# The banded attention layer of a four-layer kernel: its first 22 units issued in pairs on TensorE, and the finished heads copied one unit later

## The chip, the cores and the metric

One core of a Trainium2 chip. The kernel is timed in microseconds (us) of device time for one execution of the whole program; less is better. The kernel before has a median of 2338.8 us over 3 runs (2338.51 to 2340.18).

## The reference, cut to what matters

The program computes four mixing layers over 512 tokens of width 1024 (a dilated one, a differential one, an mLSTM with RG-LRU, and a banded attention with sinks), the last two each followed by attention over a memory and an MLP. The change touches the banded layer alone. It has 16 query heads of 64 channels, 4 key heads, and a window of 128 tokens:

```
qkv = u @ w_qkv
q, k = rotary(q), rotary(k)
# block j of 128 queries sees the keys of blocks j-1 and j
s = jnp.einsum('blkgd,bckd->bkglc', qb, kb) * scale
s = jnp.where(band, s, -inf)
m = jnp.maximum(jnp.max(s, axis=-1), sink)
p = jnp.exp(s - m[..., None])
den = jnp.sum(p, axis=-1) + jnp.exp(sink - m)
ob = jnp.einsum('bkglc,bckd->blkgd', p, vb) / den
out = ob @ w_o
```

## The kernel before

The work is written out by hand for each engine; the engines meet only at counting semaphores, and each engine takes its instructions in the order in which they are written.

**Units.** The banded layer is cut into 32 units. Unit k has head pair t = k // 4 and query block n = k % 4, so two heads of 128 queries. Its scores are 256 keys wide, or 128 where n is 0. Four kinds of work of a unit run on TensorE (PE):

- S, the scores: `unit_scores`, line 671; two matmuls of 64 rows, one for each head.
- T, the transposes of the probabilities: `transposes`, line 678; four of 128x128 (two where n is 0) into bank `TB0 + n % 2`.
- V, the values: `values` by `chain`, line 683; matmuls of 64 columns, one half of the array for each head, into bank `OB`.
- Q, a quarter of a projection tile: `quarter`, called by `between`, line 614; six matmuls 128x512 of the split product (`uh`, `ul` by `wh`, `wl`). 24 quarters make the last six tiles of the q projection, and all go through the one bank `XB`. From unit 22 on, `between` issues pieces of the output projection instead (`begin`, line 614 too).

**The order on PE** (`attend`): for each n: S(n+2), Q(n+2) or pieces, T(n), V(n-1).

**VectorE (DVE)**, in its loop over k: the masked maximum mx(k+1) (L2174), then for unit k the wait for its exponentials, the sum and reciprocal (L2891, L2893), the scaling of the probabilities (L2896) and a drain (L2897) that releases T(k). I write R(k) for the start of L2891 of unit k. Behind it come, by k % 4, the turning of the next head pair (`sw_cos`, `sw_sin`, `sw_turned`: L2180, L2186, L2189) and `result(t)` (L2882), the copy of a finished head pair from bank `OB` into `F`. V of the first unit of head pair t waits for `result(t-1)` (`y_before`). From k = 21 on DVE also makes the low parts of finished heads (`split_lo`, L2131).

**ScalarE (ACT)**, in its loop over k: ex(k+1), the exponentials (L1975, L1977); where k % 4 is 1, `take` (L1542), the copy of the tile in `XB`; pt(k), the copy of the transposes from PSUM into `spt` (L1529); where k % 4 is 1, `split_g` (L1378), two halves of a weight tile; from k = 20 on the high parts of finished heads (L1989). `spt` has two buffers, for even and odd k, and pt waits for the values that last read its buffer:

```
def spt(k): return wk(13312 + 512 * (k % 2))

def pt(U, dst, src):
    act.wait_ge(pt_psum, U + 1)
    wait(act, pv_done, U - 1)
    nc.scalar.activation(dst, src, ACT.Copy).then_inc(pt_ready, 1)
```

`pv_done` counts the units whose V is finished, so pt(k) needs T(k) and V(k-2). ACT's order is `ex(k + 1)` and then `pt(k)`. On PE, T(k) waits for pt(k-2) and V(k) for pt(k). S of a unit k up to 24 waits for mx(k-2), of a later one for mx(k-1). The first quarter of a tile waits for the `take` of the tile before it.

**GpSimd (POOL)** makes the low half of each weight tile (L573); in this layer it starts when DVE has finished the fourth unit of a head pair.

Of the kernel before, what the change touches and what calls it, by code (L numbers as in the profile page):

```python
# [27 lines left out]
TT = S // P  # L28
# [56 lines left out]
def build(nc, x, mem, positions, tiles, cols, post, consts, masks, maskd_in, rgw, out, upto="all"):  # L85
    ctx = ExitStack()
    with ctx:
# [45 lines left out]
        PS = ctx.enter_context(nc.psum_tensor("PS", [P, 8, 512], F32))  # L133
# [226 lines left out]
        def sq_(t): return wk(3072 + 512 * t)  # L360
# [246 lines left out]
        def _(pe):  # L607
# [66 lines left out]
            def transposes(U, ps, srcs, ahead=1):  # L674
                wait(pe, pt_ready, U + 1 - ahead)
                pe.wait_ge(probs_ready, U + 1)
                for n, a in enumerate(srcs):
                    last = nc.tensor.transpose(ps[:, n * P:(n + 1) * P], a, ident)  # L678
                last.then_inc(pt_psum, 1)
# [337 lines left out]
                u_ev = out_projection("diff_out", 6)  # L1017


            def attend(name, units, between=None, tiles=None):  # L1020

                U = UNIT[name]

                def values(n):
                    pe.wait_ge(pt_ready, U + n + 1)
                    wait(pe, y_taken, units[n]["y_before"])
                    for out, pairs in units[n]["values"]:
                        last = chain(out, pairs)  # L1030
                    last.then_inc(pv_done, 1)

                def unit_scores(n):
                    if "tile" in units[n]:
                        pe.wait_ge(lin_evac, units[n]["tile"])
                    if "low" in units[n]:
                        pe.wait_ge(cross_lo, units[n]["low"])
                    if "turned" in units[n]:
                        pe.wait_ge(aux_taken, units[n]["turned"])
                    if units[n].get("keys") is not None:  # L1040
                        pe.wait_ge(units[n]["keys"], 32)
                    scores(U + n, units[n]["scores"], ahead=1 if n == 0 else units[n].get("ahead", 2))

                if between is not None:
                    between(-2)
                    between(-1)
                if tiles is not None:
                    tiles(0)
                unit_scores(0)
                if tiles is not None:  # L1050
                    tiles(1)
                unit_scores(1)
                if tiles is not None:
                    tiles(2)
                for n, un in enumerate(units):
                    if n + 2 < len(units):
                        unit_scores(n + 2)
                    if between is not None:
                        between(n)
                    transposes(U + n, PS[:, TB0 + n % 2, :], un["probs"], ahead=2)  # L1060
                    if n >= 1:
                        values(n - 1)
                if between is not None:
                    between(len(units))
                values(len(units) - 1)

            if on("ev"):
# [16 lines left out]
                U = UNIT["ev"]  # L1084
# [202 lines left out]
            if on("sw"):  # L1287
                b = BASE["sw"]
                first_tiles(b, u_sw, taken=y_evac, evacuated=FF_Y0[0] + 57)
                for m in (4, 5):  # L1290
                    feature_tile(b + m, slot_of(b + m), m % 2, LIN["sw"] + m)
                    a = m - 2
                    pe.wait_ge(lin_evac, LIN["sw"] + a + 1)
                    for t in range(TT):
                        last = nc.tensor.transpose(PS[:, SV0 + a, t * P:(t + 1) * P],
                                                   svt(a)[:, t * P:(t + 1) * P], ident)
                    last.then_inc(aux_ready, 1)

                def quarter(n):

                    m, q = 6 + n // 4, n % 4
                    slot = slot_of(b + m)
                    if q % 2 == 0:
                        pe.wait_ge(lo_ready, 2 * (b + m) + q // 2 + 1)
                    if q == 0 and m > 6:
                        pe.wait_ge(lin_evac, LIN["sw"] + m)
                    for k in (2 * q, 2 * q + 1):
                        ks = slice(k * P, (k + 1) * P)
                        last = three(PS[:, XB, :], w_of(wh, slot)[:, ks], w_of(wl, slot)[:, ks],
                                     uh[:, k, :], ul[:, k, :], k == 0, k == KT - 1)  # L1310
                        if m == 11 and k < KT - 1:
                            last.then_inc(rows_read, 1)
                    if q == 3:
                        last.then_inc(tile_used, 1)

                def sw_unit(t, n):
                    l, lo = t // 2, max(n - 1, 0) * P
                    w = (n + 1) * P - lo
                    nt = w // P
                    k = 4 * t + n  # L1320
                    return dict(
                        scores=[(PS[:, sw_bank(k) + m, 0:w], sq_(t)[64 * m:64 * m + 64, n * P:(n + 1) * P],
                                 sk(l, m)[:, lo:lo + w], True, True) for m in range(2)],
                        keys=keys_mirrored[l // 2] if t % 4 == 0 and n == 0 else None,
                        probs=[ssm(k)[:, m, e * P:(e + 1) * P] for m in range(2) for e in range(nt)],
                        y_before=Y0["sw"] + t,
                        ahead=1 if k > 24 else 2,
                        turned=AUX["sw"] + t + 5,
                        values=[(PS[64 * m:64 * m + 64, OB, n * P:(n + 1) * P],
                                 [(sv[:, lo // P + e, 64 * l:64 * l + 64],  # L1330
                                   spt(n)[:, (m * nt + e) * P:(m * nt + e + 1) * P]) for e in range(nt)])
                                for m in range(2)])

                u_out = 8 * (c.add("u") - 1)

                def between(n):
                    if n < 22:
                        quarter(n + 2)
                        if n == -1:
                            pe.wait_ge(lin_evac, LIN["sw"] + 6)  # L1340
                        return
                    if n == 22:
                        pe.wait_ge(lin_evac, LIN["sw"] + 12)
                    at = (0, 1, 3, 4, 6, 9, 11, 13, 15, 17, 18, 22)[n - 22:n - 20]
                    begin(BASE["sw_out"], u_out, SW_EARLY[at[0]:at[1]], MOVED_MEM)

                attend("sw", [sw_unit(t, n) for t in range(8) for n in range(TT)], between)
                begin(BASE["sw_out"], u_out, SW_EARLY[22:34], MOVED_MEM)
            if on("ff1"):
                mlp(1, cross(1, out_projection("sw_out", 2, True)))  # L1350
# [665 lines left out]
        def _(dve):  # L2016
# [171 lines left out]
            def sw_turned(dst):  # L2188
                v.tensor_tensor(dst, stmp, dst, ALU.subtract)  # L2189
                v.drain().then_inc(aux_taken, 1)  # L2190
# [670 lines left out]
            if on("sw"):  # L2861
# [18 lines left out]
                def result(t):  # L2880
                    dve.wait_ge(pv_done, UNIT["sw"] + 4 * t + 4)
                    v.tensor_copy(F[:, t, :], PS[:, OB, :]).then_inc(y_taken, 1)  # L2882
# [3 lines left out]
                for k in range(32):  # L2886
                    if k < 31:
                        mx(k + 1)
                    w = P if k % 4 == 0 else 2 * P
                    dve.wait_ge(exp_ready, UNIT["sw"] + k + 1)  # L2890
                    v.tensor_tensor(rdn(k), den(k), sinkx(k), ALU.add)  # L2891
                    step()
                    v.reciprocal(rdn(k), rdn(k))  # L2893
                    step()
                    for m in range(2):
                        v.tensor_scalar(ssm(k)[:, m, 0:w], ssm(k)[:, m, 0:w], rdn(k)[:, m:m + 1], None, ALU.mult)  # L2896
                    v.drain().then_inc(probs_ready, 1)  # L2897
                    t = k // 4 + 1
                    if k % 4 == 0 and t < 8:
                        sw_sin(sq_(t), 4 + t)  # L2900
                    if k % 4 == 1:
                        if t > 1:
                            result(t - 2)
                        if t < 8:
                            sw_turned(sq_(t))
                    if k % 4 == 3 and t < 7:
                        sw_cos(5 + t)
                    heads = {21: (0, 1), 22: (1, 2), 23: (2, 3), 26: (3, 4), 27: (4, 5), 28: (5, 6), 30: (6, 7)}.get(k)
                    if heads is not None:
                        split_lo(*heads)  # L2910
# [174 lines left out]
```

## Time and profile before

| | |
|---|---|
| median of 3 runs | 2338.8 us (2338.51 to 2340.18) |
| the profiled execution | 2339.67 us |
| its span, first to last instruction | 2337.9 us |
| PE busy | 2293.1 us, 98% |
| DVE, ACT, POOL busy | 63%, 52%, 51% |
| mean granted TensorE clock | 0.998 |
| first scores of the banded layer | 1687.71 us |
| T(3), T(21), T(31) start | 1700.74, 1756.41, 1790.54 us |

Times inside the span are counted from its start. A row of the timeline gives the start, the duration, the engine, the line, the operation, the tiles, and in brackets the idle time in front of it and what ended it. Matmuls overlap, so the distance of two starts, and not the duration, is the time that a matmul takes from the next. A bracket is missing where the engine was not idle.

### The profile page before, as it was taken

The page shows a single profiled execution, that of the slowest core. Times are in us where ns is not written, and L with a number is a line of the kernel's source. Part 1 is how long each engine was busy: PE and PEld are TensorE (multiplying, and loading weights), DVE is VectorE, ACT ScalarE, POOL GpSimd, SP SyncE. Part 2 cuts the span into 40 slices and gives each one's busy share as a digit, 9 for nine tenths or more (in the row PEclk, how much of TensorE's full clock was granted, in tenths as well). Part 3 has the DMA queues.
Part 4 walks back from the last instruction along what each step waited for, and adds up shares of the span by engine and source line. Part 5 has one row for each costly group of instructions (what it writes and reads, how often), then busy time and mean ns, then how long its engine had stood idle before and what let it go on. Part 6 is the DMA issues. An engine that isn't in the chain of part 4 may idle for free.

```text
span 2337.9 us, 39043 instructions
## 1 busy us (share of the span) xinstructions
PE 2293.1 (98%) x13234; PEld 1907.9 (82%) x13234; DVE 1463.5 (63%) x2476; ACT 1209.9 (52%) x2606; POOL 1197.8 (51%) x834
## 2 busy tenths in 40 slices
PE   8999999999999999999999999999999999999998
PEld 7888888888877778778898988888766998988886
DVE  5554555555667776773554666787685624667686
ACT  5343334334655556654644754544576744645453
POOL 4544344442443334433662478786422742587885
PEclk9999999999999999999999999999999999999999
DMA  5333333332432222222531224233323431233331
GB/s 191 118 102 101 96 104 109 100 100 64 140 95 91 90 67 83 85 71 77 166 122 64 91 82 133 83 113 95 91 69 104 143 101 55 91 121 96 99 109 72
DMA packets 126554, 232.82 MB, mean 100 GB/s; under 512 B 17200, under 2 KB 17456, under 8 KB 126384
## 3 DMA queue, kind: packets, MB, share of 16 engines
q1 hardware_dynamic: 123536, 220.08, 29.8%
q10 hardware_dynamic: 2848, 10.49, 1.3%
q8 instruction: 105, 1.72, 0.3%
q14 instruction: 65, 0.53, 0.1%
HBM read 208.48 MB, written 2.10 MB: 90 GB/s over the span
## 4 chain that ended last, share of the span: by engine, by line
PE 64%; issue 18%; POOL 9%; DVE 5%; ACT 2%; DVEq 1%; ACTq 1%; DMA 0%; POOLq 0%
PE PS L614 56%; POOL wl L573 8%; PE PS L683 3%; PE PS L671 2%; POOL w L573 2%; PE PS L678 1%; PE PS L638 1%; DVE H L2141 1%; DVEq L2022 1%; DVE work L2174 0%; DVEq L2175 0%; DVE ul L2131 0%; ACT work L1402 0%; DMA raw<-tiles_dram 0%; DVE work L2055 0%
## 5 line engine op out<-in xcount | busy, mean ns | idle before, releaser
L573 POOL TENSOR_TENSOR wl<-raw,wh 128x512 fp32r<-128x512 f32 x502 | 716.6, 1451 | 848.9 <-ACT wh L1378 457.5
L614 PE MATMUL PS<-uh,wh 128*128 128x512 f32 (+1 forms) x2088 | 761.1, 365 | 1.9 <-DVE ul L2074 0.9
L614 PE MATMUL PS<-uh,wl 128*128 128x512 f32 (+1 forms) x2088 | 747.6, 358 | 0.0
L614 PE MATMUL PS<-ul,wh 128*128 128x512 f32 (+1 forms) x2088 | 746.9, 358 | 0.0
L614 PEld LDWEIGHTS PS<-uh,wh 128*128 128x128 f32 x2088 | 396.3, 190 | 76.8 <-issue 14.8
L614 PEld LDWEIGHTS PS<-uh,wl 128*128 128x128 f32 x2088 | 396.1, 190 | 58.2
L614 PEld LDWEIGHTS PS<-ul,wh 128*128 128x128 f32 x2088 | 396.5, 190 | 54.0 <-issue 0.5
L573 POOL TENSOR_TENSOR wl<-diagonals,wh 128x512 fp32r<-128x512 f32 x212 | 295.4, 1417 | 177.2 <-ACT wh L1378 137.5
L614 PE MATMUL PS<-wh,forms 128*128 128x512 f32 x784 | 241.3, 389 | 0.0
L1378 ACT ACTIVATE wh<-raw 128x512 fp32r<-128x512 f32 x312 | 178.7, 622 | 95.8 <-PE PS L614 84.4
L1542 ACT ACTIVATE work<-PS 128x512 f32<-128x512 f32 x120 | 71.7, 598 | 297.7 <-PE PS L614 228.9
L614 PE MATMUL PS<-wh,uh 128*128 128x512 f32 x448 | 179.3, 400 | 2.8 <-DVE ul L2131 2.7
L614 PE MATMUL PS<-wl,uh 128*128 128x512 f32 x448 | 174.9, 390 | 0.0
L614 PE MATMUL PS<-wh,ul 128*128 128x512 f32 x448 | 174.6, 390 | 0.0
L1378 ACT ACTIVATE wh<-diagonals 128x512 fp32r<-128x512 f32 x212 | 122.1, 623 | 98.9 <-PE PS L614 94.1
L614 PEld LDWEIGHTS PS<-wh,forms 128*128 128x128 f32 x784 | 147.2, 188 | 30.6
L2795 DVE TENSOR_TENSOR work<-work,PS 128x1024 f32<-128x1024 f32 x84 | 102.5, 1220 | 103.2 <-PE PS L614 101.9
L614 PE MATMUL PS<-wl,forms 128*128 128x512 f32 x392 | 152.5, 389 | 0.0
L1523 ACT ACTIVATE work<-work,stat 128x512 f32<-128x512 f32 (+3 forms) x160 | 95.6, 599 | 75.9 <-DVEq L2175 73.9
L1363 ACT ACTIVATE wh<-raw 128x512 fp32r<-128x512 f32 x190 | 109.6, 624 | 14.0 <-issue 11.4
L614 PEld LDWEIGHTS PS<-wh,uh 128*128 128x128 f32 x448 | 84.1, 188 | 25.7 <-issue 9.3
L2209 DVE TENSOR_TENSOR work<-work,cst 128x512 f32<-128x512 f32 x64 | 95.8, 1496 | 10.4 <-DMA work<-work 9.4
(278 smaller groups left out, 3512.2 us busy)
## 6 DMA issues: line engine op xcount, KB each, us to landing
raw<-tiles_dram SPq DMA_DIRECT2D x534, 256.0 KB, 2.7
diagonals<-tiles_dram SPq DMA_DIRECT2D x212, 256.0 KB, 3.0
work<-work SPq DMA_DIRECT2D x296, 64.0 KB, 2.0
gB<-post_dram ACTq DMA_DIRECT2D x8, 512.0 KB, 3.9
H<-x_dram SPq DMA_DIRECT2D x4, 512.0 KB, 5.9
H<-x_dram ACTq DMA_DIRECT2D x4, 512.0 KB, 5.2
work<-mem_dram ACTq DMA_DIRECT2D x2, 1024.0 KB, 7.2
out_dram<-H ACTq DMA_DIRECT2D x4, 512.0 KB, 2.7
```

What stands on the lines that cost most here:

```text
L573: nc.gpsimd.tensor_tensor(w_of(wl, slot)[:, hc], src[:, hc], w_of(wh, slot)[:, hc].bitcast(F32), ALU.subtract).then_inc(lo_ready, 1)
L614: last = nc.tensor.matmul(out, a, b, start=start and m == 0, stop=stop and m == 2, skip_group_check=goes_on)
L638: last = nc.tensor.transpose(half_ps(half, k, banks)[:, t * P:(t + 1) * P], xn[:, 2 * half + t, k * P:(k + 1) * P], ident)
L671: ins = nc.tensor.matmul(o, q, k, start=first, stop=last)
L678: last = nc.tensor.transpose(ps[:, n * P:(n + 1) * P], a, ident)
L683: last = nc.tensor.matmul(out, a, b, start=n == 0, stop=n == len(pairs) - 1)
L1363: nc.scalar.activation(w_of(wh, slot)[:, hc], raw[:, raw_slot, hc], ACT.Copy).then_inc(hi_ready, 1)
L1378: nc.scalar.activation(w_of(wh, slot)[:, hc], src[:, hc], ACT.Copy).then_inc(hi_ready, 1)
L1523: last = nc.scalar.activation(sm, sm, ACT.Exp, bias=bias, scale=-1.0, accum_out=d)
L1542: nc.scalar.activation(dst, PS[:, bank, 0:width], ACT.Copy).then_inc(lin_evac, 1)
L2209: v.tensor_tensor(placed(dst), plain(swp(a)), plain(sinT), ALU.mult)
L2795: v.tensor_tensor(sums[i], sums[i], region, ALU.add).then_inc(y_evac, 1)
```

## The change

`attend` gets `pairs`, and the banded layer is called with 11. For n = 0, 2, ..., 20 PE now issues S(n+2), S(n+3), then Q and T(n), Q and T(n+1), and then V(n-2), V(n-1) (none in the first pair). Unit 22 has V(20) and V(21) behind its transposes, and from there the order is as before. On DVE, `result(t - 2)` moves from the iterations k % 4 = 1 to k % 4 = 2, behind the probabilities of that unit; `sw_turned` stays. ACT, POOL and the DMA queues have no edit, and no buffer is added.

```diff
-            def attend(name, units, between=None, tiles=None):
+            def attend(name, units, between=None, tiles=None, pairs=0):
...
-                for n, un in enumerate(units):
+                for n in range(0, 2 * pairs, 2):
+                    unit_scores(n + 2)
+                    unit_scores(n + 3)
+                    for k in (n, n + 1):
+                        between(k)
+                        transposes(U + k, PS[:, TB0 + k % 2, :], units[k]["probs"], ahead=2)
+                    if n:
+                        values(n - 2)
+                        values(n - 1)
+                for n in range(2 * pairs, len(units)):
                     if n + 2 < len(units):
                         unit_scores(n + 2)
                     if between is not None:
                         between(n)
-                    transposes(U + n, PS[:, TB0 + n % 2, :], un["probs"], ahead=2)
+                    transposes(U + n, PS[:, TB0 + n % 2, :], units[n]["probs"], ahead=2)
+                    if pairs and n == 2 * pairs:
+                        values(n - 2)
                     if n >= 1:
                         values(n - 1)
...
-                attend("sw", [sw_unit(t, n) for t in range(8) for n in range(TT)], between)
+                attend("sw", [sw_unit(t, n) for t in range(8) for n in range(TT)], between, pairs=11)
...
-                    if k % 4 == 1:
-                        if t > 1:
-                            result(t - 2)
-                        if t < 8:
-                            sw_turned(sq_(t))
+                    if k % 4 == 1 and t < 8:
+                        sw_turned(sq_(t))
+                    if k % 4 == 2 and t > 1:
+                        result(t - 2)
```

## Rows read from the trace of the kernel before

**Rows 1.** Busy time by window: four units in steady state, then units 22 to 25.

```profile
1716.25:1728.60 12.35, 12.35 (x84) 8.56 (x82) 10.21 (x37) 8.91 (x31) 3.01 (x2) 1.00 0.22 64
...
1757.64:1772.34 14.70, 11.12 (x76) 7.25 (x73) 12.50 (x43) 11.22 (x36) 3.44 (x2) 1.00 0.38 126
```

**Rows 2.** Timeline of PE in steady state.

```profile
1703.99 0.38 PE L678 MATMUL PS<-cst,work 128*128 128x128 f32 x2
...
1707.55 0.44 PE L683 MATMUL PS<-work 128*64 128x128 f32 x4
1707.92 0.49 PE L671 MATMUL PS<-work 64*128 64x128 f32 x4
1708.34 0.50 PE L614 MATMUL PS<-uh,wh 128*128 128x512 f32 x1
1708.68 0.40 PE L614 MATMUL PS<-ul,wh 128*128 128x512 f32 x1
...
1709.83 0.60 PE L678 MATMUL PS<-cst,work 128*128 128x128 f32 x4
1710.36 0.67 PE L683 MATMUL PS<-work 128*64 128x128 f32 x8
1710.96 0.70 PE L671 MATMUL PS<-work 64*128 64x256 f32 x4
```

**Rows 3.** Timeline of DVE: R(0), R(1), R(2), R(11) and R(23).

```profile
1690.31 0.16 DVE L2891 TENSOR_TENSOR stat<-stat 128x2 f32<-128x2 f32 x1 [0.24 <-ACTq L1979]
...
1693.01 0.16 DVE L2891 TENSOR_TENSOR stat<-stat 128x2 f32<-128x2 f32 x1
...
1696.18 0.16 DVE L2891 TENSOR_TENSOR stat<-stat 128x2 f32<-128x2 f32 x1
...
1723.15 0.16 DVE L2891 TENSOR_TENSOR stat<-stat 128x2 f32<-128x2 f32 x1 [0.32 <-ACTq L1979]
...
1761.23 0.16 DVE L2891 TENSOR_TENSOR stat<-stat 128x2 f32<-128x2 f32 x1 [0.37 <-ACTq L1979]
```

**Rows 4.** Timeline of ACT: pt(8); take, ex(11); ex(23), pt(22).

```profile
1716.75 0.38 ACT L1529 ACTIVATE work<-PS 128x256 f32<-128x256 f32 x1 [1.09 <-PE PS L678]
...
1719.63 0.60 ACT L1542 ACTIVATE work<-PS 128x512 f32<-128x512 f32 x1 [1.11 <-PE PS L614]
...
1721.64 0.51 ACT L1975 ACTIVATE work<-work,stat 128x256 f32<-128x256 f32 x1
...
1759.72 0.50 ACT L1975 ACTIVATE work<-work,stat 128x256 f32<-128x256 f32 x1
...
1761.33 0.60 ACT L1529 ACTIVATE work<-PS 128x512 f32<-128x512 f32 x1 [0.15 <-issue]
```

**Rows 5.** Timeline of PE: the starts of T(1), T(3) and T(21).

```profile
1694.30 0.63 PE L678 MATMUL PS<-cst,work 128*128 128x128 f32 x4 [0.22 <-DVEq L2897]
...
1700.74 0.60 PE L678 MATMUL PS<-cst,work 128*128 128x128 f32 x4
...
1756.41 0.60 PE L678 MATMUL PS<-cst,work 128*128 128x128 f32 x4
```

**Rows 6.** Timeline of PE, last units: V(24), S(28), V(28), V(31).

```profile
1771.23 0.44 PE L683 MATMUL PS<-work 128*64 128x128 f32 x4
1772.34 0.49 PE L671 MATMUL PS<-work 64*128 64x128 f32 x4 [0.67 <-DVEq L2175]
...
1785.02 0.44 PE L683 MATMUL PS<-work 128*64 128x128 f32 x4
...
1794.67 0.67 PE L683 MATMUL PS<-work 128*64 128x128 f32 x8
```

**Rows 7.** Timeline of DVE, last units: R(26), R(30) and result(7).

```profile
1772.29 0.16 DVE L2891 TENSOR_TENSOR stat<-stat 128x2 f32<-128x2 f32 x1
...
1784.91 0.16 DVE L2891 TENSOR_TENSOR stat<-stat 128x2 f32<-128x2 f32 x1
...
1795.40 0.69 DVE L2882 COPY F<-PS 128x512 f32<-128x512 f32 x1 [5.03 <-PE PS L683]
```

## The prediction

> **What bounds the kernel now.** I read the page first: PE is busy 98% of the span, so what counts is what lengthens PE's own stream or makes it stand. The stretch in question is 1688 to 1795 us. By windows, four units in steady state take 12.35 us and PE is busy for 12.35 of them [rows 1]; units 22 to 25 take 14.70 with 11.12 busy. The timeline of DVE shows that PE has a partner that is nearly as full: R(k) waits for ACT only once in four units, in a gap of 0.32 us [rows 3]. A gap between two such steps is 0.20 us where nothing is late, and every fourth mx is followed by one of 0.40, so a real wait of 0.2 us is all that DVE has left in 12.35 us. In units 22 to 27 DVE leads: S(28) stood 0.67 us for its drain [rows 6]. So the two questions are what the new order costs or saves on PE, and whether it makes DVE or ACT later. The third view is ACT's: pt always stood for PE's transposes (pt(8): 1.09 us, released by L678) and never for values [rows 4]. That is what the change alters.
>
> **PE's own stream.** No matmul is added or removed; only neighbours change. From [rows 2]: a full S lasts 0.70 and a half one 0.49, so two halves of columns differ by 0.21 and S itself is 0.42; the half S is followed after 0.42, where 0.21 would do, so a change of form costs 0.21 there. V: 0.67 less 0.44 is 0.23, the half V is followed after 0.37, so 0.14 is for the change. T: 0.60 less 0.38 is 0.22 for two transposes, so four are 0.44, and V comes after 0.53: 0.09. Q's first matmul is followed after 0.34, its duration is 0.50 against 0.40 of the next: 0.10. Sum 0.54 us for a unit. A pair meets S, T-to-V and V once instead of twice; between T and Q both fill the whole array. No row here stands for S behind S or V behind V; the bounds are nothing saved and 0.54 us a pair, and I take the upper one. Eleven pairs: 6 us less work for PE. PE then needs about 12.35 - 2 x 0.54 = 11.3 us for four units.
>
> The Trainium skill, TensorEngine Tiling (Array Packing), section Tiling Modes, says the same of the mechanism: a change of tiling mode, not of tile, drains TensorE. By it the change should be faster by what the switches cost; the trace agrees with the switches but not that PE alone sets the pace, and this is the first rival below.
>
> **DVE's own stream.** Same instructions, `result` one iteration later. Behind `result` the next mx comes after one TENSOR_TENSOR step with no drain in front, so some 0.1 us may go, and with the 0.2 of waiting DVE could run four units in about 12.05 us. So even without any new wait the gain is limited to 0.3 x 4.5 = 1.4 us, not 6.
>
> **The new wait.** pt(k) needs V(k-2) finished, since `spt` has two buffers. Before, V(k-2) stands ahead of T(k) on PE, so the wait is always over. Now, for even n, V(n-2) stands behind T(n+1). T(n+1) needs probabilities of unit n+1; and on ACT pt(n) stands ahead of ex(n+2). Queued behind the waiting pt(n) are, in order: ex(n+2), take, pt(n+1), split_g, ex(n+3); DVE waits for the two ex. So a serial chain closes once a pair: T(n+1) on PE, V(n-2) on PE, pt(n) and ex(n+2) on ACT, R(n+2) and the scaling on DVE, and so on to T(n+3). Nothing hides it, for DVE had 0.2 us left.
>
> Prices of its steps. T to V: 0.53, and 0.03 more if T had stood (0.63 long against 0.60 [rows 2, 5]): 0.56. V start to a reader of its result: 1795.40 - 1794.67 = 0.73 [rows 6, 7], a half V 0.23 less, 0.50. pt: a copy of 512 columns is 0.60 long and the next starts 0.11 before its end, 0.49; of 256 columns 0.38 long [rows 4], 0.28. ex to R: 1723.15 - 1721.64 = 1.51 [rows 3, 4]; with 128 columns two activations are 0.11 shorter, 1.29. ex to ACT's next: 1761.33 - 1759.72 = 1.61. take, pt and split_g to the next ex: 1721.64 - 1719.63 = 2.01. R to T on PE: 1694.30 - 1693.01 = 1.29 [rows 3, 5]. R(4j) to R(4j+1): 1693.01 - 1690.31 = 2.70 on DVE.
>
> From T(4j+3) to T(4j+5): 0.56 + 0.50 (V(4j) is a half one) + 0.49 + 1.29 gives R(4j+4) at 2.84; DVE then needs 2.70 (ACT would be ready at 1.55 + 1.39 + 0.49 + 1.51 = 4.94, earlier than 5.54), and 1.29: 6.83 us.
>
> From T(4j+1) to T(4j+3): 0.56 + 0.73 + 0.28 = 1.57 for the start of ex(4j+2); here ACT is the slow one: + 1.61 + 2.01 + 1.51 + 1.29 = 7.99 us. DVE (R(4j+2) at 3.08 and then about 2.6 to R(4j+3) with `result`) would be ready at 5.7, ACT at 6.70.
>
> PE has time for its pair in both: V V, S S, Q, T, Q add up to 1.0 + 1.1 + 1.5 + 0.5 + 1.4 = 5.5 us behind T; only the quarter that waits for `take` (done 3.7 us after T(4j+1)) comes near, and then T(4j+3) could start at 7.1, before 7.99. POOL starts when the fourth unit is ready, and its 3.0 us now lie beside DVE's idle time; I cost that at nothing, up to 0.6 us in four units in favour.
>
> Four units: 6.83 + 7.99 = 14.8 us instead of 12.35. The first pair has no V and no wait: R(2) stays at 1696.18 [rows 3], S(5) needs mx(3) just before it, and 0.63 + 1.49 + 0.45 + 1.38 puts T(3) at 1700.1, against 1700.74 [rows 5]: 0.6 us ahead. From T(3) to T(21) there are five intervals of 6.83 and four of 7.99, 66.1 us, where the trace has 1756.41 - 1700.74 = 55.67. T(21) is late by 66.1 - 55.7 - 0.6 = 9.8 us.
>
> The pair of unit 20 closes the chain once more, with one high part behind pt(20) and two behind split_g (copies of 512 columns, 0.5 each by the row of take): R(23) comes at 1.57 + 0.5 + 1.61 + 2.01 + 1.0 + 1.51 = 8.2 us after T(21); before 1761.23 - 1756.41 = 4.8. So 3.4 more, 13.2 in all.
>
> **The moved copy.** While V(n-2) stands behind T(n+1), the copy one iteration later is early enough. From unit 22 on the old order holds, and V(24) stands on PE right behind T(25) but needs result(5), which is now behind the probabilities of unit 26. R(26) is at 1772.29 [rows 7], 0.61 earlier without the copy; drain and copy end 1.2 + 0.7 later, 1773.6; V(24) was at 1771.23 and S(28) behind it at 1772.34 [rows 6]. With 0.37 for V, S(28) is at 1774.05: 1.7 us late, and PE has no idle time in the rest of that run. V(28) likewise needs result(6) behind R(30) (1784.91 + 1.7 - 0.6 + 1.9 = 1787.9) and was at 1785.02 + 1.7 = 1786.7: 1.2 us more. Bounds: 0 if DVE is that much ahead of PE by then, 2.9 if not. I take 2.9, since both copies hang on DVE's own chain. T(31), and with it the projection behind, moves by the whole sum; from T(31) on PE's order is unchanged, and what follows waits for PE.
>
> **Sum.** 9.8 + 3.4 + 2.9 = 16.1 us. The profiled execution, 2339.67, becomes 2355.8; it lies 0.9 above the median of the runs, so the forecast for the median is 2338.8 + 16.1 = 2355 us, slower by 0.7%.
>
> **Rivals.**
> - PE alone sets the pace, and waits stay away: faster by 6 us, 2332.8. It needs pt not to be held and DVE to have 1 us of slack in four units. For it: PE is 12.35 of 12.35. Against: DVE's 0.2 us. It decides only if the chain from T(n+1) to T(n+3) is under 5.6 us; my lower sum is 6.8. Chance 0.05.
> - The chain does not bind but DVE does: 1.4 us gained, 2.9 lost by the moved copy, 2340.3, no change. Against: the code of pt. Chance 0.07.
> - The chain binds and the moved copies cost nothing: 2352. Chance 0.08.
> - The clock falls because PE stands 20% of the time. Units 22 to 25 kept 1.00 at 11.12 of 14.70 busy [rows 1], which speaks against. At half clock PE's 5.6 us for a pair would be 11.3, 3.9 more than 7.4, over ten pairs near 39 us: 2394. Chance 0.03.
> - The forecast: 0.77.
>
> Own range of the forecast: each interval of the chain is off by 0.2 at most, ten of them 2 us; POOL's overlap up to 2.5 in favour; tail 0 to 4. That is 2349 to 2360, which takes in the third case too: 0.85 of the chance, so this is the range given. About 0.2% is what a measurement of this kernel can tell from no change. Slower by more: 0.77 + 0.08 + 0.03 = 0.88; same 0.07; faster 0.05.
>
> **What the profile of the changed kernel would show.** The waits of ACT: L1529 released by V (L683), about 1.2 us behind T(n+1), once a pair, which never occurs before. Windows of four units of 14.8 us with PE busy for 11.5 or so. DVE idle in front of L2891, released by ACT. T(21) near 1766. V(24) and V(28) behind a DVE copy, L2882. S S and V V without a gap. I would be wrong if L1529 is still released by L678 alone, or if the windows of four units stay near 12 us; if they are right and the total is not, the tail is mis-sized. The likeliest wrong size is the interval with take and split_g, where ACT's work could fit elsewhere.

## The result and the profile after

The changed kernel takes 2356.88 us, median of 4 runs (2354.5 to 2358.86), beside 2338.66 us for the kernel before (4 runs). The ratio is 1.0076, with a 95% interval of 1.0059 to 1.0094: slower by 18 us, where 2355 was forecast. The profiled execution took 2354.5 us with a span of 2352.7.

Runs of one kernel differ by some microseconds in places that have nothing to do with this layer, so I compare a length inside the layer: from the first scores to the start of T(31). It is 1790.54 - 1687.71 = 102.83 us before and 1805.40 - 1685.88 = 119.52 us after, 16.69 us more. The layer's first scores come 1.83 us earlier in the profiled execution of the changed kernel, in code that is the same. From T(31) to the end both need 547.3 us. So the 14.8 us between the two spans are 16.69 from the layer less 1.83 of the run's own, and the layer explains the loss.

In the new file DVE's and ACT's lines are numbered about 11 higher: pt is L1540, take L1553, the exponentials L1986, the sum behind R(k) L2902, the drain of the probabilities L2908, `result` L2893.

The page's first part and the clock of the changed kernel, as percentages of its span and in tenths:

```profile
PE 2292.8 (97%) x13234; PEld 1909.8 (81%) x13234; DVE 1457.5 (62%) x2476; ACT 1209.8 (51%) x2606; POOL 1197.8 (51%) x834
...
PEclk9999999999999999999999999999999999999999
```

Over the whole span PE's busy time has hardly moved, and within the layer neither (96.79 us before, 96.89 after, by windows): what the pairs save is offset, at least in part, by a stretch at the border to the single units in which TensorE's clock was at its lower level (see "The border" below). Four units in steady state, by windows, beside [rows 1]:

```profile
1705.22:1720.13 14.91, 11.94 (x83) 8.56 (x83) 9.46 (x37) 8.88 (x31) 3.00 (x2) 1.00 0.18 54
```

14.91 us instead of 12.35, at a full clock, and all engines have idle time; PE is busy for 11.94 of them. Who waits for whom, from 1688 to 1812 us (total, times, longest):

```profile
ACT work L1540 <- PE PS L683: 29.0, 10, 3.3
DVE stat L2902 <- ACTq L1990: 18.8, 16, 1.9
...
ACT work L1540 <- PE PS L678: 15.2, 9, 3.0
...
PE PS L678 <- DVEq L2908: 9.4, 11, 1.6
PE PS L614 <- ACT work L1553: 7.6, 5, 2.3
...
PE PS L683 <- DVE F L2893: 3.7, 3, 2.4
```

The first row is the answer. ACT's copy of the transposes waits for values (L683) exactly ten times, once for each pair behind the first; before, it waited for transposes alone [rows 4]. DVE waits for ACT and PE waits for DVE: that is the whole ring. One turn of it, on PE:

```profile
1705.22 0.63 PE L678 MATMUL PS<-cst,work 128*128 128x128 f32 x4 [1.04 <-DVEq L2908]
1705.78 1.14 PE L683 MATMUL PS<-work 128*64 128x128 f32 x16
1706.85 1.01 PE L671 MATMUL PS<-work 64*128 64x128 f32 x8
...
1713.25 0.63 PE L678 MATMUL PS<-cst,work 128*128 128x128 f32 x4 [0.60 <-DVEq L2908]
```

on ACT:

```profile
1706.56 0.38 ACT L1540 ACTIVATE work<-PS 128x256 f32<-128x256 f32 x1 [3.28 <-PE PS L683]
1706.84 0.50 ACT L1986 ACTIVATE work<-work,stat 128x256 f32<-128x256 f32 x1
...
1708.45 0.60 ACT L1553 ACTIVATE work<-PS 128x512 f32<-128x512 f32 x1 [0.15 <-issue]
...
1710.46 0.51 ACT L1986 ACTIVATE work<-work,stat 128x256 f32<-128x256 f32 x1
```

and on DVE:

```profile
1708.35 0.16 DVE L2902 TENSOR_TENSOR stat<-stat 128x2 f32<-128x2 f32 x1 [1.36 <-ACTq L1990]
...
1711.97 0.16 DVE L2902 TENSOR_TENSOR stat<-stat 128x2 f32<-128x2 f32 x1 [1.17 <-ACTq L1990]
```

T(5) starts at 1705.22, the values behind it at 1705.78; pt(4) has stood 3.28 us and starts at 1706.56, 1.34 us behind T(5). R(6) follows at 1708.35, R(7) at 1711.97 behind ACT's long turn (take, pt, the weight tile, the exponentials), and T(7) at 1713.25: 8.03 us for the pair. The other pair takes 6.86 to 6.88 (T(3) 1698.36 to T(5) 1705.22). The rows count two for each matmul of S and V: V(2) and V(3) are eight matmuls in the kernel and x16 here.

At the end of the layer, V(24), V(28), T(30) and T(31):

```profile
1785.67 0.44 PE L683 MATMUL PS<-work 128*64 128x128 f32 x4 [2.41 <-DVE F L2893]
...
1799.88 0.44 PE L683 MATMUL PS<-work 128*64 128x128 f32 x4 [1.10 <-DVE F L2893]
1801.74 0.60 PE L678 MATMUL PS<-cst,work 128*128 128x128 f32 x4
...
1805.40 0.63 PE L678 MATMUL PS<-cst,work 128*128 128x128 f32 x4 [1.57 <-DVEq L2908]
```

V(24) and V(28), the first values of their head pairs, now stand for the moved copy.

### The profile page after: what moved, and what is told of

The parts are those of the page before. It is cut to its first block, busy times and chain, and to the rows that moved or that the text cites. A ratio compares the mean times of both kernels' runs of the same rounds, so it can differ in the third digit from the quotient of the medians.

```text
span 2352.7 us, 39043 instructions
## 1 busy us (share of the span) xinstructions
PE 2292.8 (97%) x13234; PEld 1909.8 (81%) x13234; DVE 1457.5 (62%) x2476; ACT 1209.8 (51%) x2606; POOL 1197.8 (51%) x834
## 3 DMA queue, kind: packets, MB, share of 16 engines
q8 instruction: 105, 1.72, 0.3%
## 4 chain that ended last, share of the span: by engine, by line
PE 61%; issue 19%; POOL 9%; DVE 5%; ACT 2%; ACTq 2%; DVEq 1%; DMA 0%; POOLq 0%
PE PS L614 54%; POOL wl L573 8%; PE PS L683 2%; PE PS L671 2%; POOL w L573 2%; PE PS L678 1%; ACTq L1990 1%; PE PS L638 1%; DVE H L2152 1%; DVE work L2185 1%; DVEq L2033 1%; DVEq L2186 0%; DVE ul L2142 0%; ACT work L1413 0%; DVE work L2907 0%
## 5 line engine op out<-in xcount | busy, mean ns | idle before, releaser
L1553 ACT ACTIVATE work<-PS 128x512 f32<-128x512 f32 x120 | 71.8, 598 | 292.8 <-PE PS L614 223.2
```

The source lines that it names most:

```text
L1553: nc.scalar.activation(dst, PS[:, bank, 0:width], ACT.Copy).then_inc(lin_evac, 1)
```

## The experiments

T(21) and T(31) are read from one profiled execution of each kernel, in us from the first scores of the layer; "ratio" is the time of all runs against the kernel before on the same chip, with its 95% interval.

| kernel | T(21) | T(31) | ratio |
|---|---|---|---|
| before | 68.70 | 102.83 | |
| changed | 78.97 | 119.52 | 1.0076 (1.0059 to 1.0094) |
| e1, tail copies back | 78.94 | 116.89 | 1.0059 (1.0047 to 1.0071) |
| e2, four buffers | 66.48 | 105.85 | 1.0011 (1.0003 to 1.0020) |
| e3, copy moved alone | 77.05 | 115.74 | 1.0051 (1.0031 to 1.0070) |
| e4, values between | 68.11 | 102.58 | 0.9999 (0.9990 to 1.0007) |
| e5, values between, ACT copies | 70.94 | 106.10 | 1.0013 (1.0004 to 1.0022) |
| e6, four buffers, tail back | 66.47 | 101.29 | 0.9986 (0.9977 to 0.9995) |
| e7, e6 with ACT copies | 65.15 | 100.30 | 0.9990 (0.9981 to 1.0000) |
| e8, six pairs | 74.81 | 108.89 | 1.0025 (1.0015 to 1.0034) |
| e9, e7 up to unit 18 | 65.13 | 99.97 | 0.9986 (0.9977 to 0.9995) |
| e10, result(4) at 21 | 65.18 | 101.83 | 0.9997 (0.9988 to 1.0006) |
| e11, buffers alone | 68.70 | 102.79 | 0.9994 (0.9985 to 1.0004) |

### e1: the copies of the tail back in their old place

```diff
+                    if k > 24 and k % 4 == 1 and t > 1:
+                        result(t - 2)
                     if k % 4 == 1 and t < 8:
                         sw_turned(sq_(t))
-                    if k % 4 == 2 and t > 1:
+                    if k < 24 and k % 4 == 2 and t > 1:
                         result(t - 2)
```

> The changed kernel, but the finished heads that are copied in the iterations 26 and 30 are copied in 25 and 29 again, as before; the copies up to iteration 22 stay moved. Theory (the moved copy costs 2.9 us in the unpaired tail): first scores of the layer to T(31), 119.5 us in the changed kernel, becomes 116.6; no stall of V(24) and V(28) behind the copy; total about 2354, 0.65% over before. Rival (the copies are hidden by DVE's own lead and the tail is late for another reason): T(31) stays at 119 to 120 us and the stall in front of V(24) is replaced by an equal one in front of S(28) or T(31).

Measured: T(31) at 116.89, 2.63 us earlier than in the changed kernel (2.9 worked out), T(21) the same to 0.03. Median 2353.53 us, where about 2354 was expected. Neither V(24) nor V(28) stands for the copy any more. So the moved copy costs about what the rows said, and only in the single units at the end. The 0.27 us that is missing is left open; in this run the clock was at its lower level for 3.4 us from 1779.0 us.

### e2: four buffers for the copied transposes

```diff
-        def spt(k): return wk(13312 + 512 * (k % 2))
+        def spt(k): return wk(13312 + 512 * (k % 4))
...
-            def pt(U, dst, src):
+            def pt(U, dst, src, buffers=2):
                 act.wait_ge(pt_psum, U + 1)
-                wait(act, pv_done, U - 1)
+                wait(act, pv_done, U + 1 - buffers)
...
-                    pt(UNIT["sw"] + k, spt(k)[:, 0:2 * w], PS[:, TB0 + k % 2, 0:2 * w])
+                    pt(UNIT["sw"] + k, spt(k)[:, 0:2 * w], PS[:, TB0 + k % 2, 0:2 * w], buffers=4)
```

> The changed kernel with four buffers for the copied transposes of the banded layer, so that pt(k) waits for V(k-4) and no longer for V(k-2); nothing else differs. Theory (the wait of pt for the values behind the second transposes closes a serial chain): four units fall from 14.91 to about 12.1 us, where DVE is full, pt waits for transposes alone; the stretch to T(31) is that of before plus 2.9 for the moved copies less 1.4, about 104.5 us, total within 0.1% of before. Rival (the pairs themselves are slow, since PE's transposes of the first of a pair come late or a score is late for DVE): four units stay over 13.5 us. Rival (PE alone set the pace before): four units fall to 11.3 us.

Measured, by windows, four units, and then a stretch of 3.4 us:

```profile
1711.36:1723.41 12.05, 11.62 (x84) 8.71 (x83) 10.22 (x37) 9.14 (x32) 3.01 (x3) 1.00 0.23 68
1772.80:1776.20 3.40, 3.40 (x10) 2.53 (x9) 2.06 (x9) 0.00 (x0) 1.58 (x1) 0.52 0.00 0
```

Four units are 12.05 us, as the theory has it, with the same pairs and the same order on every engine. Of the ten waits of pt for values (29.0 us) the profile shows one left, of 0.43 us, and T(21) is 2.2 us ahead of before. This settles the main point: the loss between T(3) and T(21) is the wait for a buffer. It also shows that PE's saving is real but capped, for PE is idle 0.43 us of 12.05.

T(31) was 1.3 us later than expected. V(24) stood 2.44 us for the copy, and 0.8 us behind it (1772.9) TensorE's granted clock fell to its lower level, 1.2 GHz, for 3.4 us: the second row, a window that begins 0.1 us before the fall, has 0.52, and the pieces of the projection started 0.43 us apart instead of 0.23:

```profile
1771.68 0.44 PE L683 MATMUL PS<-work 128*64 128x128 f32 x4 [2.44 <-DVE F L2893]
...
1773.55 0.63 PE L614 MATMUL PS<-wh,uh 128*128 128x512 f32 x1
1773.98 0.63 PE L614 MATMUL PS<-wh,ul 128*128 128x512 f32 x1
```

### e3: the copy moved alone, no pairs

```diff
-                    if k % 4 == 1:
-                        if t > 1:
-                            result(t - 2)
-                        if t < 8:
-                            sw_turned(sq_(t))
+                    if k % 4 == 1 and t < 8:
+                        sw_turned(sq_(t))
+                    if k % 4 == 2 and t > 1:
+                        result(t - 2)
```

> The kernel before with only the copy of finished heads moved from the iterations k % 4 = 1 to k % 4 = 2, no pairs. Theory (in the old order V of the first unit of a head pair stands right behind the transposes of that unit and waits for the copy behind the next unit's probabilities): PE stands about 2 us in front of that V in each four units, four units take about 13.7 us instead of 12.35, and the kernel is slower than before by 8 to 11 us, 2348. Rival (the moved copy costs only where PE has no other work, 2.9 us in the tail): 2341.6.

Measured: 12.9 us more to T(31), above the 8 to 11 expected, and a median of 2352.6 us where 2348 was. Four units take 13.7 to 14.0, where 13.7 was worked out, but the first four (T(5) to T(9)) took 16.3, with the clock at its lower level for 3.4 us from 1710.6; a second such stretch began at 1782.3. V of the first unit of a head pair stands for the copy seven times, for 1.1 to 2.4 us where about 2 was expected; for instance:

```profile
1724.12 0.44 PE L683 MATMUL PS<-work 128*64 128x128 f32 x4 [1.23 <-DVE F L2882]
```

So the copy may be moved only together with the pairs, whose values are late enough for it. In e2, where it is moved too, four units are 12.05.

### e4: the values between the two transposes

```diff
                         transposes(U + k, PS[:, TB0 + k % 2, :], units[k]["probs"], ahead=2)
-                    if n:
-                        values(n - 2)
-                        values(n - 1)
+                        if n and k == n:
+                            values(n - 2)
+                            values(n - 1)
```

with the copies as in e1.

> The changed kernel with V(n-2) and V(n-1) issued between T(n) and T(n+1) instead of behind T(n+1), two buffers as before, and the copies of iterations 26 and 30 back in 25 and 29. Theory (the place of V(n-2) behind T(n+1) is the whole loss; the pair's merged scores and values are a gain on PE that DVE caps): pt waits about 0.7 us for values and that is hidden, four units take about 12.05 us, the stretch to T(31) is 101.5 us, total 2337.5, faster by 0.05% or the same. Rival (a pair of scores in front of the quarter delays T(n) enough to hold ACT and DVE): four units 12.6 us or more, 2340 or more.

Measured: four units take 11.8 to 12.5 us, 12.16 in the mean from T(5) to T(21), and T(31) is at 102.58, 1.1 later than expected. pt still waits for values ten times, for 0.3 to 1.6 us where about 0.7 was expected (11.9 us in all), but now at a place where most of it costs nothing. Without another buffer, only by an order in which V(n-2) stands ahead of T(n+1), the loss is gone (0.9999). It is the same as before and not faster; in this window PE is busy for 12.03 of 12.05 us:

```profile
1727.48:1739.53 12.05, 12.03 (x83) 8.88 (x82) 10.00 (x37) 8.88 (x31) 2.80 (x3) 1.00 0.21 63
```

In this order V stands between two full-array stretches, one change of form more than in the pair.

### e5: e4 with the finished heads copied by ACT

```diff
+                    if k > 24 and k % 4 == 1:
+                        copy_head(k)
                     if k < 31:
                         ex(k + 1)
+                    if 4 < k < 24 and k % 4 == 2:
+                        copy_head(k)
...
-                    if k % 4 == 2 and t > 1:
-                        result(t - 2)
```

where `copy_head` waits for `pv_done` and copies bank `OB` into `F`.

> The kernel with the values between the two transposes, and the first seven finished heads copied by ACT instead of DVE (iterations 6, 10, ... 22 ahead of the copy of the transposes, 25 and 29 ahead of the exponentials). Theory (without the wait DVE sets the pace, PE needs only 11.3 us for four units): four units fall from 12.05 to about 11.5 us, the stretch to T(31) from 102.58 to 98.5 us, total 2335 to 2336, 0.15% under before. Rival (ACT or PE's switches hold it): four units stay at 12.0 us or over, total as before.

Measured: four units 12.85 us, T(31) 106.10, median 2342.83 us. The theory fell. The copy waits its turn on ACT, and the first values of the next head pair wait for it, since here they stand only one transpose behind:

```profile
1711.18 0.90 PE L683 MATMUL PS<-work 128*64 128x128 f32 x12 [1.06 <-ACT F L2004]
```

### e6: e2 with the copies of e1

> The changed kernel with four buffers for the copied transposes and the copies of iterations 26 and 30 back in 25 and 29. Theory (chain and moved tail copies are the whole loss): four units 12.05 us, stretch to T(31) about 100.6 us (2.2 under before), total 2337, 0.1% under before. Rival (something else in the pairs delays the tail, as the 5.2 us between T(21) and T(31) in the run with four buffers alone might say, where 2.9 was worked out): the stretch stays over 103 us.

Measured: T(31) at 101.29, 1.54 us ahead of before and 0.7 later than expected; a median of 2337.57 us beside 2340.12 for the kernel before, ratio 0.9986, with an interval that excludes no change (1.2 to 5.4 us faster, so the layer's 1.54 is near its lower end). Its window of four units, and the place where e2 lost its clock (V(24), S(28)):

```profile
1713.44:1725.49 12.05, 11.60 (x84) 8.72 (x83) 10.22 (x37) 9.12 (x32) 3.02 (x3) 1.00 0.25 73
```

```profile
1771.24 0.44 PE L683 MATMUL PS<-work 128*64 128x128 f32 x4
1772.33 0.49 PE L671 MATMUL PS<-work 64*128 64x128 f32 x4 [0.66 <-DVEq L2186]
```

V(24) no longer stands and the clock stays. Chain, moved tail copies and the clock behind them are the whole of the loss; e2 is 4.56 us later than e6 at T(31): 3.24 of it arises between T(25) and T(26), where V(24) stands and the clock falls, and 1.18 between T(29) and T(30), where V(28) stands.

### e7: e6 with the copies on ACT

The edit of e5 on e6.

> The changed kernel with four buffers for the copied transposes and the first seven finished heads copied by ACT instead of DVE. Theory (DVE is the next bound): four units about 11.4 us, stretch to T(31) about 97 us, total 2333 to 2334, 0.2% under before. Rival (PE is the next bound already at 12 us, its forms cost more than worked out from rows): four units stay at 12.0 us.

Measured: four units 11.55 to 11.69 us up to T(19), T(21) at 65.15, 1.3 ahead of e6; but T(22) to T(23) took 6.83 us instead of 4.07, with the clock halved for 3.4 us there, and T(31) is at 100.30, where 97 was expected. The ratio, 0.9990, is no better than that of e6. DVE was the next bound, and by only 0.4 to 0.5 us in four units.

### e8: six pairs

```diff
-between, pairs=11)
+between, pairs=6)
```

with the copy moved for k < 12 alone.

> The changed kernel with 6 pairs instead of 11 (units 0 to 11), the copy moved only for units under 12 and in its old place behind. Theory (each pair behind the first closes the chain once, 1.2 us a pair): T(11) comes 4.5 us later in the layer than before, T(31) about 5.3 us later (108.1 us after the first scores), total 2344, 0.22% over before. Rival (the loss is at the border between pairs and single units, or in the tail): T(11) and T(31) are both late by over 10 us, or T(11) is not late.

Measured: T(11) 42.27 instead of 37.72, 4.55 late; T(31) 6.06 late, where 5.3 was expected: the border to the single units adds 1.5, all of it up to T(14), which is 6.09 late. Median 2346.14 us. In pairs four units take 14.92, behind them 12.3:

```profile
1715.15:1730.07 14.92, 11.94 (x83) 8.56 (x83) 9.47 (x37) 8.88 (x31) 3.02 (x3) 1.00 0.18 55
1744.03:1756.33 12.30, 12.30 (x84) 8.60 (x82) 9.98 (x37) 8.88 (x31) 2.77 (x3) 1.00 0.24 71
```

The loss goes by the pair, with some more once at the border, and the single units give none of it back.

### e9 and e10: ACT copies only up to unit 18

The copy of ACT is limited to `4 < k < 20`; DVE makes result(4) in iteration 22 (e9) or 21 (e10).

> Four buffers for the copied transposes, pairs, and the first four finished heads (iterations 6, 10, 14, 18) copied by ACT; result(4) in iteration 22 and the rest as in the run e6 on DVE. Theory (the gain of the ACT copies, 11.6 us for four units instead of 12.04, was lost at unit 22, where ACT also makes three high parts of heads and PE then stood long enough for its clock to be halved): T(21) comes 65.2 us after the first scores, T(31) at 100.0 us, total 2336, 0.17% under before. Rival (the tail waits for something that does not depend on T(21)): T(31) stays at 101.3 us, total as e6.

> As e9, with result(4) on DVE in iteration 21, as in the kernel before, instead of 22. Theory (at the border to the single units DVE is the chain, so the place of a copy on it shifts nothing unless PE waits for it): T(31) within 0.4 us of e9. Rival (V(20) waits for result(4) in iteration 22): T(31) 0.4 to 0.8 us earlier than in e9.

Measured, four units of e9 by windows:

```profile
1715.05:1726.62 11.57, 11.57 (x84) 8.71 (x82) 9.51 (x36) 9.45 (x33) 2.90 (x3) 1.00 0.21 60
```

T(31) of e9 is at 99.97, 1.3 ahead of e6, as expected, and PE is busy all the time, so it is the bound again. It then needs 11.57 to 11.67 us, 0.3 more than the 11.3 worked out. The total, 2336.87 us beside 2340.66 (0.9986), can't be told from e6. In e10 both expectations were wrong: T(22) came 2.4 us later and the clock was halved, because the copy in iteration 21 has to wait for V(19), which the last pair puts behind T(21):

```profile
1753.47 0.69 DVE L2896 COPY F<-PS 128x512 f32<-128x512 f32 x1 [1.91 <-PE PS L683]
```

### e11: four buffers alone

The edit of e2 on the kernel before.

> The kernel before with four buffers for the copied transposes and nothing else. Theory (in the old order V(k-2) is always ahead of T(k), so the wait that the buffers relax never bound): no change, T(31) 102.8 us after the first scores, four units 12.35 us, ratio within 0.1% of 1. Rival (the buffers help by themselves, and part of the gain of e6 is theirs): T(31) under 102.

Measured: T(31) at 102.79 against 102.83, ratio 0.9994 with 1 inside its interval. The buffers do nothing by themselves in the layer, so the 1.54 us that e6 gains there are the pairs'. The ratios alone (0.9986 and 0.9994) could not show this, since their intervals overlap.

## Why the prediction was right

The mechanism was the one forecast: pt(n) waits for V(n-2) behind T(n+1), and the wait closes a ring through PE, ACT and DVE once a pair. Its size came out right nearly step by step. One of the prices was lucky, as said below, and the time was forecast 0.6 us short in the layer.

**PE's own stream.** Worked out: 0.54 us saved for a pair. Measured in the changed kernel: V V take 1.07 (1705.78 to 1706.85), S S 1.06 (from 1699.75 to the first quarter at 1700.81); added up with quarters and transposes, two full units need 5.97 us where two of before need 6.5, 0.53 less. For full units the upper bound was the right one. Over four units, half ones among them, less is reached: in e9, where PE sets the pace, they take 11.57 to 11.67 us, 0.7 to 0.8 less than before, where 1.08 was worked out. Part of the rest is a wait of 0.14 us in front of T(9), which starts 0.37 us behind the last product instead of 0.23 and has no bracket. The windows of the changed kernel were to show PE busy for 11.5 us or so and show 11.94; that difference is not split up here. In the forecast this term did not count, since DVE capped it.

**DVE's floor.** Worked out: about 12.05 us for four units without any new wait. e2 and e6 have 12.03 to 12.05 (T(7) to T(11), for one), and in e2's windows of four units DVE waits for ACT in front of no R(k).

**The new wait.** Worked out: 6.83 and 7.99 us for the two kinds of pair. Measured: 6.86 and 8.03. From T(5) to T(7) the steps were 0.56 to V(2), 0.78 to pt(4) (0.73 worked out), 0.28 to ex(6), 1.61 to `take`, 2.01 to ex(7), 1.51 to R(7) and 1.28 to T(7).

In the other pair one price was right by luck. The 2.70 us from R(4j) to R(4j+1) were read at unit 0. In the steady state of the kernel before the same step takes 3.47 (R(12) to R(13)), because the scaling of a half unit's probabilities takes 1.16 us there, beside POOL's step on the weight tile, and 0.48 where POOL is idle:

```profile
1690.79 0.48 DVE L2896 TENSOR_SCALAR work<-work,stat 128x128 f32<-128x128 f32 x2
...
1726.56 1.16 DVE L2896 TENSOR_SCALAR work<-work,stat 128x128 f32<-128x128 f32 x2
```

```profile
1724.43 3.01 POOL L573 TENSOR_TENSOR wl<-diagonals,wh 128x512 fp32r<-128x512 f32 x2 [9.34 <-DVEq L2897]
```

In the changed kernel DVE stands 1.9 us for ACT in front of R(4), POOL's step ends meanwhile, and the scaling takes 0.48 in every half unit; so R(4) to R(5) is 2.71. The prediction gave no reason for the smaller price, and named a gain from POOL's overlap, up to 0.6 in four units, on top, which its 2.70 already contained. With 3.47 the pair would have been worked out at 7.6 and T(21) 3.9 us later than forecast.

T(3) was forecast 0.6 ahead and was 0.55 (12.48 against 13.03 from the first scores). T(21) was forecast 9.8 late and was 10.27. e2 removes the wait and with it all of this; e4 removes it by order; e8 about halves it with about half the pairs.

**The border.** Worked out: R(23) 8.2 us behind T(21), 3.4 more than before. Measured: 1773.16 - 1764.85 = 8.31, 3.5 more. Counted from the first scores, R(23), R(24) and R(25) all come 13.75 to 13.76 us later than before, and T(25) 13.79. T(23) itself is 15.2 late. TensorE stood 2.27 us for `take` there and its clock then was at the lower level from 1770.6 to 1777.4 us:

```profile
1773.16 0.16 DVE L2902 TENSOR_TENSOR stat<-stat 128x2 f32<-128x2 f32 x1 [0.66 <-ACTq L1990]
```

```profile
1769.25 0.50 PE L614 MATMUL PS<-wh,uh 128*128 128x512 f32 x1 [2.27 <-ACT work L1553]
```

```profile
1770.60:1777.40 6.80, 6.35 (x27) 4.43 (x26) 5.26 (x15) 4.76 (x17) 2.96 (x2) 0.50 0.64 188
```

That cost T(23) some 1.8 us, seen against e1, where the clock was still full and T(23) came at 88.89 instead of 90.67. It cost DVE's chain nothing: R(24) is at 91.80 in the changed kernel and at 91.76 in e1, and DVE leads in these units.

**The moved copy.** Forecast 1.7 and 1.2; T(26) is 1.72 later against T(25) than before, and T(31) 1.18 later against T(26). e1 took back 2.63 of these 2.90.

**The rivals.** PE alone (faster by 6): excluded by the ring of waits, and by e2, where PE gains no more than DVE lets it. DVE alone (no change): that is nearly e2, 1.0011, so it was the right account of a kernel without the wait. Moved copies at no cost (2352): excluded by the rows of V(24) and V(28) and by e1. The clock: it did fall, for 6.8 us in the changed kernel, but at the border; in the pairs it stayed at 1.00 with PE busy for 11.94 us of 14.91. The 39 us were far off.

**The total.** 9.8, 3.4 and 2.9 were forecast, 16.1 in sum; 10.27, 3.52 and 2.90 were measured, 16.69 in the layer, and 18.2 between the medians of 4 runs, with an interval from 13.8 to 22. The 1.5 between layer and median is inside that interval and I leave it unexplained.

## What to carry to other kernels

When work is regrouped on one engine, look at what another engine's next instruction waits for before it may reuse a buffer: moving V(n-2) behind T(n+1) turned a wait that never bound into a ring through three engines. Either the buffers grow with the group (e6: ratio 0.9986, 1.54 us gained in the layer) or the release stays ahead of the next producer (e4: no loss). Where two engines are both full, a saving on one is capped by the slack of the other, here 0.3 us in 12.35 until the copy left DVE.

## What the runs showed of the hardware

In this layer TensorE's clock fell to the lower level for 3.4 us at a time (once 6.8) around places where PE stood: from 1772.9 us in e2 behind 2.44 us of standing, from 1770.6 in the changed kernel, 1779.0 in e1, 1710.6 and 1782.3 in e3, 1764.9 in e5, 1760.0 in e7 and 1757.7 in e10. It did not follow every such wait: V(24) of the changed kernel stood 2.41 us and the clock stayed, V(24) of e2 stood 2.44 and it fell. In code that is the same in all kernels such stretches appear in some executions and not in others: near 610 us in e4, e6, e7, e8 and e9, near 1656 us in e1 and e2 (in e9 at 1661.0), near 963 us in all but e1 and e2. In such a stretch a matmul of 512 columns takes 0.20 us more (0.43 against 0.23 us), so 3.4 us of it cost PE some 1.6 (an estimate: about eight such matmuls).

A change of form on PE, between 64-row, 64-column and full-array matmuls, costs 0.09 to 0.21 us, 0.53 us for a pair of full units when it is avoided. Between transposes and full-array products there was none: in e9 two transposes and the first product behind them take 0.45 us, and the rows of the kernel before have 0.22 for two transposes and 0.23 for a product:

```profile
1718.99 0.38 PE L678 MATMUL PS<-cst,work 128*128 128x128 f32 x2
1719.13 0.48 PE L614 MATMUL PS<-uh,wh 128*128 128x512 f32 x1
1719.44 0.40 PE L614 MATMUL PS<-ul,wh 128*128 128x512 f32 x1
```

In the kernel before DVE's scaling of a half unit took 0.48 us where POOL was idle (units 0, 24 and 28) and 1.16 to 1.17 beside POOL's step (units 4 to 20). The low part of a head, 128x512 on DVE, took 0.69 us and beside POOL's step 1.77.
